# Three passes over the tokens instead of two in a fused decoder step, with the samples' state products on VectorE

## The reference

```
proj = x @ w_in                                   # 2048 -> z, xbc, dt, u/v, gates
y_a  = ssd_branch(z, xbc, dt, conv, state, ...)   # causal conv, SiLU, chunked scan: 8 groups of 8 heads
y_b  = chunk_sgu_branch(uv, ...)                  # gelu, layer_norm(v), 128x128 mix inside each chunk
merged = sig(ga) * (y_a @ w_branch_a) + sig(gb) * (y_b @ w_branch_b)
h = layer_norm(DN_ALPHA * x + merged @ w_out)
y = layer_norm(DN_ALPHA * h + peer(h))

# scan, per chunk of 128 tokens: y = (C B^T * decay) (dt x) + C state ; state = decay * state + B^T (dt x)
# for a sample token: state = exp(dt A) * state + (dt x) B^T ; y = sum_n state[.., n] * C[n]

def peer(h):                                      # 8 heads, 128 x 128 product keys, top 16 each
    s = (h @ w_q) . sub_keys ; best 16 of the 16 x 16 sums -> 16 experts and gates per head
    return sum_{head,k} gate * gelu(h . u_tab[e]) * v_tab[e]   # 128 rows of u and 128 rows of v per token
```

## Time and profile before

| | us |
|---|---|
| median of 3 runs | 5419.52 (5419.21 to 5420.57) |
| profiled execution, its own time | 5416.87 |
| its span | 5414.9 |

### The profile page before, as it was taken

One profiled execution on the slowest core, in us unless ns is written; L12 is line 12 of the kernel. 1 busy time (PEld: TensorE's weight loads), 2 busy tenths in 40 slices (PEclk: granted clock), 3 DMA queues, 4 the chain that ended last, 5 costly groups with the idle time before them and its releaser, 6 DMA issues. The chain is left out here.

```text
span 5414.9 us, 43573 instructions
## 1 busy us (share of the span) xinstructions
PE 3608.6 (67%) x16560; PEld 3028.1 (56%) x16560; DVE 3422.2 (63%) x4133; ACT 702.4 (13%) x1501; POOL 2398.3 (44%) x1504
## 2 busy tenths in 40 slices
PE   7999979999999968888778697897940000230000
PEld 5787768888887757667667586786740000000000
DVE  3455531000001859989867665565798999789999
ACT  2232321000000123333311010000100000000000
POOL 3575730000000025545543432443318888778885
PEclk8999989999999989999889898998975555565555
DMA  5565643344444379999989899999749999999998
GB/s 175 192 217 196 210 156 132 133 148 164 164 156 140 126 301 405 421 420 410 421 356 377 351 421 384 389 421 412 307 155 398 420 422 422 422 380 422 422 422 363
DMA packets 275097, 1672.07 MB, mean 309 GB/s; under 512 B 37041, under 2 KB 66225, under 8 KB 81969
## 3 DMA queue, kind: packets, MB, share of 16 engines
q0 software_dynamic: 161920, 1133.78, 51.2%
q1 hardware_dynamic: 112968, 535.51, 26.4%
HBM read 1633.31 MB, written 35.79 MB: 308 GB/s over the span
## 5 line engine op out<-in xcount | busy, mean ns | idle before, releaser
L250 POOL DMA_INDIRECT rows_a<-in_peer_u,expert x384 | 819.0, 2133 | 2182.4 <-POOLq L369 1149.2
L409 PE MATMUL psum<-rows_a,w_ring 128*128 128x264 f32 x7168 | 1625.5, 388 | 24.1 <-PEq L369 18.9
L409 PEld LDWEIGHTS psum<-rows_a,w_ring 128*128 128x128 f32 x7168 | 1367.2, 191 | 265.5 <-issue 30.5
L409 PE MATMUL psum<-x_acts,w_ring 128*128 128x256 f32 x5632 | 1257.4, 384 | 131.0 <-PEq L369 57.5
L409 PEld LDWEIGHTS psum<-x_acts,w_ring 128*128 128x128 f32 x5632 | 1084.0, 193 | 287.9 <-issue 83.4
L306 DVE SCALAR_TENSOR_TENSOR rows_a<-rows_a,h_tokens 128x2048 f32<-128x2048 f32 x384 | 878.7, 2289 | 106.1 <-DMA rows_a<-in_peer_u,expert 75.9
L250 POOL DMA_INDIRECT rows_a<-in_peer_v,expert x384 | 593.3, 1545 | 333.2 <-DVE h_tokens L327 165.1
L327 DVE SCALAR_TENSOR_TENSOR h_tokens<-rows_a,coef,h_tokens 128x2048 f32<-128x2048 f32 x256 | 602.6, 2354 | 79.4 <-issue 73.5
L1744 PE MATMUL psum<-acc,selector 8*128 8x512 f32 x64 | 57.5, 1075 | 683.8 <-DVE rows_a L306 479.0
L1744 PEld LDWEIGHTS psum<-acc,selector 8*128 8x128 f32 x64 | 19.9, 325 | 720.0 <-DVE rows_a L306 485.3
L1019 DVE SCALAR_TENSOR_TENSOR conv_acc<-raw,g_par,conv_acc 128x256 f32<-128x256 f32 x288 | 175.5, 609 | 283.8 <-ACT conv_acc L913 277.0
(11 more groups left out here) (368 smaller groups left out, 3024.8 us busy)
## 6 DMA issues: line engine op xcount, KB each, us to landing
w_ring<-in_w_tiles SPq DMA_DIRECT2D x448, 1024.0 KB, 6.3
smp_state<-in_state_ssm POOLq DMA_DIRECT2D x64, 256.0 KB, 5.7
out_ssm_sample<-smp_state POOLq DMA_DIRECT2D x64, 256.0 KB, 3.1
rows_a<-acum_rows_dram SPq DMA_DIRECT2D x16, 512.0 KB, 7.4
BC_bcast<-smp_bc_dram POOLq DMA_DIRECT2D x8, 1024.0 KB, 5.0
branch_b<-acum_rows_dram SPq DMA_DIRECT2D x16, 512.0 KB, 12.4
rows_a<-in_peer_u,expert POOLq DMA_INDIRECT x384, 20.6
rows_a<-in_peer_v,expert POOLq DMA_INDIRECT x384, 21.1
```

What stands on the lines that cost most here:

```text
L250: return pool.indirect_dma_start(out=dst, out_offset=None, in_=table, in_offset=bass.IndirectOffsetOnAxis(ap=self.index(s), axis=0))
L409: last = pe.matmul(o, self.w_ring[:, p % RING, k * P:(k + 1) * P], x[:, k, :], start=start and k == 0, stop=stop and k == KB - 1)
```

## The change

- `PASS_CHUNKS`: three passes. The first has chunk 0 and the samples (136 columns), the second chunk 1 (128), the third chunks 2 and 3 (256). All 224 weight tiles are read a third time.
- The ring has four tiles in the first two passes and three in the last (`RINGS`, `w_more`).
- `plan`: the experts of block 0 run in the second pass, 80 steps (4 in each scan group, 48 behind); 180 steps run in the third (10 in each scan group, 100 behind). `tail` keeps the same steps.
- In a pass with one chunk the second chunk's scan work is gone from each group, `chunk_b` stands behind the last z tile, and the next group's first `conv` stands behind the gating product.
- Samples: the loads of states move from GpSimd's queue to SP's, between the weight loads (`load_smp`); the product with C moves from GpSimd to VectorE, ahead of its sum.

```diff
-RING = 3
-PASSES = 2
-CP = CH // PASSES
-NP = CP * P
+PASS_CHUNKS = ((0, 1), (1, 1), (2, 2))
+PASSES = len(PASS_CHUNKS)
+RINGS = (4, 4, 3)
...
+STEPS_B = (4, 4, 7, 8, 4, 8, 7, 2, 8)
+STEPS_C = (10, 12, 14, 22, 12, 22, 10, 2, 6)
...
+        for i, (scan, v, u, gate, wb, wa, mix, ln, q) in ((1, STEPS_B), (2, STEPS_C)):
+            for g in range(G):
+                put(i, [("ssd", g, c) for c in range(9)], scan)
...
+                def load_smp(v):
+                    if ps.smp and 0 <= v < NU * G:
+                        if v >= 4:
+                            sp.wait_ge(st_out[v % 4], 16 * (v // 4))
+                            sp.wait_ge(prod_read, v - 3)
+                        sp.dma_start(sst[:, v % 4], state_in[GT * (v // NU) + v % NU // 2, :,
+                                                             HB * (v % 2):HB * (v % 2) + HB, :]).then_inc(st_in[v % 4], 16)
...
-                        self.load_weight(sp, pos(g, t) + RING)
+                        self.load_weight(sp, pos(g, t))
+                        if t >= 3 and NU * g + t - 3 >= 4:
+                            load_smp(NU * g + t - 3)
+                        if t == 0 and g > 0:
+                            load_smp(NU * g - 1)
...
-                        dve.wait_ge(prod_ready, v + 1)
+                        dve.wait_ge(smp_ready, v + 1)
+                        dve.wait_ge(bc_in, 16 * (g + 1))
+                        o(dve.tensor_tensor(sout[:, v % 2], sst[:, v % 4], Cb[:, b0:b0 + HB, :], ALU.mult))
...
+                    if nc_ == 1 and g < G - 1:
+                        conv(g + 1, 0)
...
+                            pool.sem_inc(smp_ready, 1)
                             pool.dma_start(state_out[GT * g + t, :, b0:b0 + HB, :], s).then_inc(st_out[v % 4], 16)
-                            if v >= 2:
-                                pool.wait_ge(prod_read, v - 1)
-                            pool.tensor_tensor(sout[:, v % 2], s, Cb[:, b0:b0 + HB, :], ALU.mult).then_inc(prod_ready, 1)
```

More of the change, by code:

```diff
@@ L69 @@
 N_GROUPS = N_TILES - FT
-RING = 3
-PASSES = 2
-CP = CH // PASSES
-NP = CP * P
+PASS_CHUNKS = ((0, 1), (1, 1), (2, 2))
+PASSES = len(PASS_CHUNKS)
+RINGS = (4, 4, 3)
+RING = max(RINGS)
+BLOCK_PASS = [i for i, (first, count) in enumerate(PASS_CHUNKS) for _ in range(count)]
 GP_B = CT * 4
@@ L454, in steps, with span @@
     def steps(self, ps, *key):
-        return self.at[key] if ps.i == 1 else ()
-    def span(self, *names):
-        every = [s for key, r in self.at.items() if key[0] in names for s in r]
-        return range(min(every), max(every) + 1)
+        return self.at.get((ps.i,) + key, ())
+    def span(self, ps, *names):
+        return [s for key, r in self.at.items() if key[0] == ps.i and key[1] in names for s in r]
     def build(self):
@@ L477, in build @@
         passes = [Pass(i) for i in range(PASSES)]
+        ring = [p % RINGS[p // N_TILES] for p in range(PASSES * N_TILES)]
+        last, self.w_slot, self.w_turn, self.w_held, self.loaded = {}, ring, [], [], 0
+        for p, slot in enumerate(ring):
+            self.w_held.append(last.get(slot, -1))
+            self.w_turn.append(ring[:p].count(slot))
+            last[slot] = p
         self.pass_a = passes[0]
@@ L1147, in _ @@
                         ex.v_row(pool, s)
-                    for s in self.span("ssd"):
-                        ex.rows(pool, s, 4, 4)
+                if ex:
+                    for s in self.span(ps, "ssd"):
+                        ex.rows(pool, s)
                 if ps.smp:
@@ L1293, in _ @@
                 def _(pool):
-                    for s in self.span("v", "u"):
-                        ex.rows(pool, s, 4, 4)
+                    for s in self.span(ps, "v", "u"):
+                        ex.rows(pool, s)
             @block.tensor
@@ L1473, in _ @@
                 def _(pool):
-                    for s in self.span("gate", "wb", "wa", "out", "ln", "q"):
-                        if s < SLOTS:
-                            ex.u_row(pool, s + 4)
-                        ex.v_row(pool, s + 4 - ex.lag)
+                    for s in self.span(ps, "gate", "wb", "wa", "out", "ln", "q"):
+                        ex.rows(pool, s)
             @block.tensor
@@ L1487, in _ @@
                     project(P_GA + m, G_GA + m, xs)
[L1488 removed]
+                if pick:
                     pe.wait_ge(smp_in, 32)
@@ L1601, in _ @@
                 for c in range(2 * FT):
-                    if not ps.smp and c == 2:
+                    if pick and c == 2:
                         for s in range(2):
```

321 lines of the change are left out of this document (162 added, 159 removed).

## The result

| | us |
|---|---|
| before, median | 5420.05 (5419.21 to 5421.02) |
| changed kernel, median | 5661.89 (5651.95 to 5665.43) |
| ratio | 1.0443, 95% interval 1.0425 to 1.0461 |
| profiled execution after, its own time and span | 5651.95 and 5650.1 |

The account below looks back on a forecast made before the run. First pass bound by TensorE, second pass and tail by transfers. Tables and passes 56 + 1172 + 1150 + 1900, tail 1348, sum 5626 us, less 25: span 5600, median 5605, 3.4% slower; range 5425 to 5730.

Parts of the forecast that it names:

- Price of a tile: TensorE's time for a weight tile goes with the columns: 3.6 us at 128 columns, 3.8 at 136.
- First pass, scan: First pass's scan: a group falls from 86.6 to 65 us, the scan from 723 to 545, set by GpSimd's chain.
- closing chain: First pass's scan group, behind the units: product, sum, gating, square, `rms`, next tiles, transposes; 26.2 us become 16.6.
- B and C to DRAM and back, unchanged: Start of each scan group in the first pass: this transfer keeps its 8.3 us.
- First pass, rest: First pass behind the scan: `sgu` 147, gates and branches 304, output, norm and query tiles; sum 627 us for 1132.
- Second pass: New second pass, priced by bytes: scan 440, `sgu` 160, gates 125, branches 197, output and norm 98, query 130; 1150 us.
- Third pass: Last pass, 256 columns with fewer expert steps: scan 715 us, sum 1900, from 2156.
- The 25 us taken off: Whole kernel: 25 us subtracted from the parts' 5626 because the single allowances for stalls can't all be due.
- fifth case: Whole kernel: the forecast itself, 5430 to 5740 us; chance 0.72.
- The faster case: All passes: idle time goes as transfers are spread, passes of 1110, 1025 and 1823 us, total 5362; chance 0.15.
- The clock: First two passes: TensorE at 1.2 GHz for part of the time, +150 us, total 5755; chance 0.06.
- The slow product: First two passes: 128-column products take 191 ns instead of 112, 6.1 us a tile, total 6280; chance 0.03.

Follow-up runs that it names:

- e_two_smp: Two-pass kernel before with only the samples' change: states loaded by SP, product with C on VectorE; 5412.98 us, ratio 0.9991.
- e_smp_pool: Three-pass changed kernel with the samples' change taken back: GpSimd loads the states and multiplies by C; 5756.52 us.
- e_load_pool: Three-pass changed kernel with only the state loads back on GpSimd, product with C still on VectorE; 5705.83 us.
- e_ring3: Three-pass changed kernel with a ring of three weight tiles in all passes; 5720.12 us.

## Why the prediction was right, point by point

**What bounds what.** Right in the main. The first pass's scan hangs on GpSimd's chain (taking the samples' edit back costs 91 us there), its other stages on TensorE, the second pass on the transfers (4.2 us a step at a DMA share of 0.95), the third on TensorE with the transfers near. Transfers aren't all of it in the second pass: without the rows' bytes it loses 139 us and still takes 1002, with TensorE busy for 882. The tail is 1348 us in both. One sign of being right was missed by a little: the scan group was to take 60 to 70 us and takes 71.1 (70.2 in the mean).

**Price of a tile.** Right: 80 tiles of the first pass in 306 us are 3.83 each, forecast 3.8; 3.74 at 128 columns, forecast 3.6. The loads of 32 weights in 3.65 us beside them are 114 ns each in step with the products. One load lasts 190 to 192 ns in these stages too; that isn't how often one can start. The prediction's own reading of the earlier trace rows was loose: by it the four loads of the mix start 0.14 us apart (985.24 to 985.80), and not 0.11, which would have made 4.5 us a tile; the 0.11 us are the products'. The rule of the Trainium skill (TensorE: Matmul & The Clock Gate, Part 3, "The mechanism"), read as the prediction read it, would have every load wait for the products ahead of it and give some 225 ns; the trace doesn't agree, now in bursts of 32. The same section names a second case beside the other row group, the background weight buffer, which the prediction passed over; with that case the 114 ns agree.

**First pass, scan: the term that was mis-sized.** Forecast 65 us a group, 545 in all; measured 71.1 (70.2 in the mean) and 579. The units (40.5, measured 39.5) and the closing chain (16.6, measured 16.2) were right. The step "B and C to DRAM and back, unchanged" was wrong: 15.4 instead of 8.3 us. I took the price of a transfer from a stage where the queues carried 197 GB/s, and put it in one whose tiles are worked through almost twice as fast. Inside one broadcast (355 to 375) the changed kernel moves this, in the view of the transfers (issues, KB each, us to landing):

```profile
DMA packets 3155, 6.70 MB, mean 335 GB/s; under 512 B 195, under 2 KB 2382, under 8 KB 2510
...
smp_state<-in_state_ssm SPq DMA_DIRECT2D x4, 256.0 KB, 8.2
BC_bcast<-smp_bc_dram POOLq DMA_DIRECT2D x1, 1024.0 KB, 10.1
```

GpSimd's two waits of the broadcast, all eight groups together, show who has which part:

| form | waits, us |
|---|---|
| two passes, samples as before (before) | 49 |
| two passes, state loads on SP (`e_two_smp`) | 55 |
| three passes, samples as before (`e_smp_pool`) | 80 |
| three passes, state loads on GpSimd (`e_load_pool`) | 83 |
| three passes, ring of three (`e_ring3`) | 91 |
| three passes, the change | 98 |

With the samples' work the same, three passes add 30 us to the 49; the fourth tile, a part of that, has at most 7. The state loads on SP add 6 in two passes and 15 in three. So the larger part comes with the narrower pass. What it has beside the broadcast is the weights at 3.8 us a tile instead of 7.1; that it is these transfers, and not something else of the narrower pass, is argued and wasn't tested apart.

**First pass, rest.** 627 forecast, 618 measured.

**Second pass.** The scan's bytes were exact (405 us at 408 GB/s are 165 MB, the forecast's number), but the 27 us that I added for its start weren't due; `sgu` took 177 for 160, with the stream at 333 GB/s and TensorE at 137 us of 177, and gates and branches took 337 for 322. These errors cancel, which is luck: 1140 for 1150.

**Third pass.** Every stage within 12 us, in sum 1909 for 1900.

**The 25 us taken off.** Wrong. "The single allowances for stalls can't all be due" had no row behind it; the parts summed to 5626 and the span is 5650. The forecast of 5600 for the span was 50 us short: these 25, the scan's 34, and 9 the other way in all other terms. With the 7 us of the median below, the change came out 57 us dearer than forecast, 242 for 185. Left alone, the sum would have missed the span by 24.

**Median and profiled run.** I carried the 4.6 us of before over. The changed kernel's runs spread from 5652 to 5665, its median is 11.8 above the span.

**Small slips.** By the earlier trace rows TensorE is busy for 1756 us in the first pass and 1742 in the second, where the prediction has 1755 and 1743, and its fifth case and its range name two pairs of bounds (5430 to 5740, 5425 to 5730). Nothing hangs on either.

**Rivals.** The faster case (1110, 1025, 1823) needed both later passes to lose their idle time. They kept it, at 1141 and 1909. Without the rows' bytes they take 1002 and 1832, close to that case, so it is these transfers that keep the passes from it. The clock: the granted clock of the second pass is 0.92, and that of the scan of the first 0.80, between the two levels of 1.2 and 2.4 GHz. The latter lies in a stage where TensorE waits anyway. The slow product didn't occur.

## What to carry to other kernels

A pass over fewer rows halves only what goes with the rows; before splitting, look in the stage's timeline for the chain that doesn't (here a broadcast and units of fixed length) and price the transfers on it under the traffic that the new stage will have, not under that of the old. The same edit can be worth nothing in one form (6 us of 723) and much in the next (91 of 670), so time it in the form it is meant for, and look whether it shortened the chain at all: moving the state loads behind the weight tiles left the units at 53.3 us with 264 columns, because the tiles come at TensorE's pace. Movable work is best spread by its marginal price in each stage, which two runs with another split show (here 4.2 and 1.3 us a step, then 2.8 and 1.8, each give or take 0.25 by the spread of the passes), and not by counting bytes alone.

## What the runs showed of the hardware that I had not expected

- The landing of one 1 MB broadcast from GpSimd's queue took 5.0 us (median) in before, whose scan moved 197 GB/s in all, and 9.3 in the changed kernel, whose scan moved 235 GB/s in the mean and 335 around one broadcast; with the broadcast in two halves the first half was used 7.5 us after its issue. The Trainium skill (DMA: Bandwidth & Descriptors, "Anatomy of one DMA") gives about 2 us and the bytes at 436 GB/s, an estimate of 4.4 us by that page for 1 MB. The trace of before agrees roughly; that of the changed kernel doesn't, beside other transfers.
- The same DMA share stands for different rates. Stages whose transfers are almost all weight tiles move some 350 GB/s for a full share (283 at 0.80, 248 at 0.70 in the first pass), stages with 8 KB rows among them 403 to 411 (371 at 0.92 over the second pass, 408 at 1.00 in its scan); with 512-byte rows the second pass is back at 351 (263 at 0.75).
- Weight loads that last 191 ns each start every 114 ns, beside products that start every 117 ns, for 32 instructions in a row, and tile after tile: 80 tiles of 136 columns in 306 us are 120 ns an instruction.
